# Two mixer layers: a mean in front of half a modulation product, rows copied earlier, two sums of squares in front of another half

## The reference

```python
mod_x = (silu_c @ w_mod[l] + b_mod[l])            # six vectors of 1024: sh1 sc1 gt1 sh2 sc2 gt2
hx = modulate(rms_norm(x, g_norm1[l]), sh1, sc1)
out_x = token_mixer(hx, ...)                      # below
x = x + gt1 * out_x
x = x + gt2 * channel_mixer(modulate(rms_norm(x, g_norm2[l]), sh2, sc2))

def token_mixer(h, p, ...):
    a_val, a_gate, s_bg, s_cg, s_x, c_x, c_g = split(h @ p['w_in'])
    u = conv_a(a_val * sigmoid(a_gate), p['conf_w'], ...)       # 31 taps
    ya = silu(layer_norm(u, ...))                               # mean and variance over 256 channels
    yb = s_bg * conv_b(s_cg * s_x, ...)
    hf, hb = rglru_bidir(c_x, ...)                              # gates, two scans
    yc = (hf + hb) * gelu(c_g)
    y = head_rms_norm(concatenate([ya, yb, yc]), p['g_mix'])    # mean square over heads of 64
    return y @ p['w_out'], ...
```

## Time and profile before

| | before |
|---|---|
| device time, median of 3 runs | 1575.61 us (1571.6 to 1576.92) |
| the profiled execution, device time | 1575.62 us |
| its span in the trace | 1573.5 us |
| TensorE busy | 1485.1 us (94%) |
| VectorE busy | 838.6 us (53%) |
| ScalarE busy | 617.6 us (39%) |
| mean granted TensorE clock | 0.972 |

### The profile page before, as it was taken

The page is one execution under the profiler, slowest core; times in us unless marked ns, Lnnn a source line. Parts: engine busy times, 40 slices in busy tenths (PEclk is TensorE's granted clock), DMA queues, the critical chain, the costliest instruction groups (busy, mean ns, idle before and its releaser), DMA issues.

```text
span 1573.5 us, 21947 instructions
## 1 busy us (share of the span) xinstructions
PE 1485.1 (94%) x8714; PEld 1046.4 (67%) x8715; DVE 838.6 (53%) x1135; ACT 617.6 (39%) x698; POOL 17.4 (1%) x56
## 2 busy tenths in 40 slices
PE   5999798999999999897869999999999999999997
PEld 3886487788888887783745566565666557555764
DVE  2899945333333323798553554445554555545553
ACT  3426723322122222549243333334444444434442
POOL 2000000000000000100010000000000000000000
PEclk8999999999999999899989999999999999999998
DMA  9633933922533133347259999989999999999992
GB/s 359 194 107 111 329 124 135 226 74 57 151 107 91 55 109 124 107 135 275 84 216 346 329 337 328 339 322 407 380 408 407 400 389 398 409 376 406 382 409 110
DMA packets 208007, 395.44 MB, mean 251 GB/s; under 512 B 12045, under 2 KB 123041, under 8 KB 207905
## 3 DMA queue, kind: packets, MB, share of 16 engines
q1 hardware_dynamic: 207312, 393.80, 69.8%
q10 hardware_dynamic: 592, 0.21, 0.1%
HBM read 392.93 MB, written 1.05 MB: 250 GB/s over the span
## 4 chain that ended last, share of the span: by engine, by line
PE 87%; ACT 4%; DMA 4%; DVE 3%; issue 2%; DVEq 0%; ACTq 0%; SPq 0%
PE bank L754 86%; DMA raw<-in_w_mod 2%; PE bank L1244 1%; DMA raw<-in_moe_w 1%; DVE tb L1824 1%; ACT la L1528 1%; DVE h_lo L1832 0%; ACT lr L1522 0%; PE bank L1189 0%; DMA rows_sb<-in_b_mod 0%; PE bank L779 0%; ACT li L1524 0%; ACT lm L1535 0%; ACT w_hi L1407 0%; ACT lr L1530 0%
## 5 line engine op out<-in xcount | busy, mean ns | idle before, releaser
L2261 DVE TENSOR_TENSOR w_lo<-raw,w_hi 128x2048 fp32r<-128x2048 f32 x132 | 302.4, 2291 | 265.8 <-ACT w_hi L1649 263.0
L1649 ACT ACTIVATE w_hi<-raw 128x2048 fp32r<-128x2048 f32 x132 | 252.4, 1912 | 409.6 <-PE bank L754 282.4
L754 PE MATMUL bank<-h_hi,w_hi 128*128 128x512 f32 (+1 forms) x768 | 285.7, 372 | 13.8 <-DVE h_lo L1832 11.8
L754 PE MATMUL bank<-h_lo,w_hi 128*128 128x512 f32 (+1 forms) x768 | 283.6, 369 | 0.0
L754 PE MATMUL bank<-h_hi,w_lo 128*128 128x512 f32 (+1 forms) x768 | 283.6, 369 | 0.0
L1407 ACT ACTIVATE w_hi<-raw 128x2048 fp32r<-128x2048 f32 (+1 forms) x64 | 113.7, 1776 | 211.1 <-PE bank L754 197.7
L754 PEld LDWEIGHTS bank<-h_hi,w_hi 128*128 128x128 f32 x768 | 147.2, 192 | 39.6 <-DVE h_lo L1832 13.4
L754 PEld LDWEIGHTS bank<-h_lo,w_hi 128*128 128x128 f32 x768 | 147.5, 192 | 23.6
L754 PEld LDWEIGHTS bank<-h_hi,w_lo 128*128 128x128 f32 x768 | 147.4, 192 | 23.7
L754 PE MATMUL bank<-w_hi,hc_hi 128*128 128x512 f32 (+1 forms) x384 | 153.8, 401 | 2.5 <-ACT warm L1704 2.5
L1807 DVE TENSOR_TENSOR w_lo<-raw,w_hi 128x2048 fp32r<-128x2048 f32 (+1 forms) x64 | 135.9, 2123 | 36.5 <-ACT w_hi L1407 36.3
(11 more groups left out here) (307 smaller groups left out, 1803.3 us busy)
## 6 DMA issues: line engine op xcount, KB each, us to landing
raw<-in_moe_w SPq DMA_DIRECT2D x220, 1024.0 KB, 8.7
raw<-in_w_mod SPq DMA_DIRECT2D x48, 1024.0 KB, 8.3
raw_x<-in_moe_w SPq DMA_DIRECT2D x44, 1024.0 KB, 8.7
raw<-in_ffn_w SPq DMA_DIRECT2D x44, 512.0 KB, 5.3
raw<-in_w_in SPq DMA_DIRECT2D x18, 1024.0 KB, 5.4
raw<-in_ffn_w SPq DMA_DIRECT2D x16, 704.0 KB, 4.5
raw<-in_w_out SPq DMA_DIRECT2D x8, 1024.0 KB, 5.7
x_in<-in_ctx SPq DMA_DIRECT2D x1, 1024.0 KB, 5.0
```

Source lines behind the costliest of these rows:

```text
L754: return nc.tensor.matmul(dst, lhsT, rhs, start=first, stop=last)
L1649: nc.scalar.activation(w_hi[:, j % SPL, :], raw[:, E_SLOT[j], :], ACT.Copy)\
L2261: V.tensor_tensor(w_lo[:, j % SPL, :], raw[:, E_SLOT[j], :], w_hi[:, j % SPL, :].bitcast(F32), ALU.subtract).then_inc(dve_done, dve_n(name ...
```

## The change

Four edits in the two mixers. No instruction is added or taken away.

1. In layer 1, at gate 4, the mean of the convolution's output comes ahead of the first half of vector 3 on TensorE, not behind it.
2. In layer 0 VectorE copies the rows of vectors 2 and 3 one tile earlier, in tile (1, 1), ahead of the LayerNorm's product (L2096).
3. In layer 1 VectorE copies them two tiles earlier, in tile (1, 0).
4. In both layers TensorE sums the squares of tiles 4 and 5 ahead of the second half of vector 5; tiles 6 and 7 stay behind it.

```diff
                     if q == CONF_AT[l]:
                         head_sums(l, ts, HEAD_SUM[0], (2, 3))
-                    if (l, q) == (1, 4):
-                        modulation(*MIX_MODS[l][0][1], range(2))
                     if q == MEAN_AT[l]:
                         pe.wait_ge(*evacuated(("w_in", l, WIN_ORDER[-1])))
                         pe.wait_ge(dve_done, at("conf_u", l))
                         for v in range(2):
                             i = mm(STAT[:, ts], ones_d[:, :].to_broadcast([P, P]), y[:, v, ts], v == 0, v == 1)
                         i.then_inc(pe_done, pe_n("conf_mean", l))
+                    if (l, q) == (1, 4):
+                        modulation(*MIX_MODS[l][0][1], range(2))
...
                 for i8 in range(4):
                     head_factor(l, ts, i8)
+                head_sums(l, ts, HEAD_SUM[1], (4, 5))
                 modulation(*MIX_MODS[l][1][1], range(2, MOD_K))
-                head_sums(l, ts, HEAD_SUM[1], (4, 5, 6, 7))
+                head_sums(l, ts, HEAD_SUM[1], (6, 7))
...
-                        if (d, t) == (1, 2):
+                        if (d, t) == (1, 1 - l):
                             dve.wait_ge(pe_done, at("used", "mod", *MIX_MODS[l][0][1], MOD_K - 1))
                             for m in MIX_MODS[l][0]:
                                 mod_row(*m)
```

## The result

The changed kernel took 1567.9 us (median of 9 runs, 1566.3 to 1569.72) against 1574.03 us before (9 runs, 1571.17 to 1576.92): a ratio of 0.9958, 95% interval 0.9946 to 0.997, or 6.1 us by the medians and 6.6 us by the ratio (4.7 to 8.5 us by its interval). The forecast was 1571.8 us, 4.0 us less, with 1569.0 as the lower end of its range. The direction was right; the size was too small by about 2 us, and the time fell out of the range.

What follows compares the result with a forecast made beforehand. TensorE, busy 1485.1 of 1573.5 us, was taken as the bound, so only idle or low-clock time could be won. Gains of 2.8 + 1.2 = 4.0 us gave 1571.6, stated as 1571.8 us, range 1569 to 1576.

Steps and rivals of the forecast that it cites:

- The chain: Both mixers: late rows delay vector 4, that delays vector 5's last load, and that the sums and ScalarE's squares (8.27 us idle).
- Layer 1, 2.8 us (2.4 to 3.0): Layer 1's mixer: the first w_out product starts at about 757.3 instead of 760.13, 2.8 us gained.
- the slow sums of tiles 0 and 1: Layer 1, behind the pause: these sums (0.60 us) take up to 0.3 us more at low clock.
- Layer 0, 1.2 us: Layer 0's mixer: first product 0.4 us later, a low-clock stretch worth 1.7 us goes; net 1.2 us gained.
- 0.92 us more at half clock: Layer 0: sums of tiles 0 and 1 take 0.92 us longer, moving tile 7 from 192.60 to 193.5.
- The low-clock stretch: Layer 0, 196.2 to 199.6 at clock 0.50: expected to go because TensorE works without a gap; costs 1.7 us.
- The sum: Whole kernel: 2.8 us from layer 1 plus 1.2 us from layer 0, 4.0 us gained.
- Whatever these two starts gain is kept: After 760.13 (layer 1) and 195.32 (layer 0) TensorE has long product stretches ahead, so gains there stay.
- the clock moves elsewhere in the layers between: Between the mixers: listed as one sign that the prediction is wrong, with no size given.
- The slower one: After the longer pauses TensorE stays at 1.2 GHz through both stretches: 9 us lost, 1584.8 us; chance 0.04.
- More than forecast: Both mixers: new bursts start at full clock and later drops go too, over 4.7 us gained, 1570.5 us; chance 0.1.

Runs made afterwards that it cites:

- the rows alone: Kernel before with only the row copies moved, one tile sooner in layer 0 and two in layer 1: 1572.17 us, ratio 0.9991 to before.
- The delays: Changed kernel plus unread matmuls of 512, 512 + 256 or 3 x 512 columns in layer 0's w_out product: 1568.7, 1570.13 and 1571.36 us.
- the warm pause: Changed kernel plus unread matmuls (6 in layer 0, 8 in layer 1) before the sums of tiles 0 and 1: 1570.18 us, ratio 0.998 to before.

## Why the prediction was right and wrong

**The chain was read rightly.** Late rows, late vector 4, late load, late squares: all four links moved as described. The columns of layer 1 follow the last gate at once, the last chunk of vector 5 is there in time, ScalarE's 8.27 us wait is gone, and the product waits for tile 7.

**Edit 1** gave ScalarE its 0.80 us; the mean waited 0.67 us for the convolution's last tap, as the estimate had it. What the forecast did not see is that this is worth little without edit 4 (50.70 against 50.89 us).

**Layer 1, 2.8 us (2.4 to 3.0).** Against the profile that the forecast was made from it was 52.90 - 49.52 = 3.38 us, against the two later profiles of before 2.0 to 2.2 us. The mechanism was right, and the 2.8 us lie between the two. Part of the base was particular to the profile read: the low-clock stretch from 756.0, which the two later profiles of before do not have. Two details were off: the first product was set by tile 7 alone, not by TensorE's burst, and the slow sums of tiles 0 and 1 cost 0.1 us (0.70 against 0.60), not the 0.3 I allowed.

**Layer 0, 1.2 us.** The first product was to come 0.4 us later. In the profile it came 0.13 us sooner after the first square; beside the two later profiles of before it came 0.2 us later. The step at fault is "0.92 us more at half clock": the sums took 1.13 us instead of 0.92, because those 0.92 us were mostly the wait for the second square, not work. The low-clock stretch went as forecast, worth 1.56 us. The reason given, TensorE at work without a gap, is not shown: with the rows alone this stretch ran at full clock too, though TensorE had waits of 0.59 and 1.08 us right ahead of the first product, as before.

**The sum.** In the profiles the two mixers gave 3.38 + 1.56 + 0.13 = 5.1 us, or, from the later profiles of before, 2.1 + 1.55 - 0.2 = 3.4 us; the forecast of 4.0 lies between. This is the part that the sum had terms for.

**What failed is that the sum ended there.** "Whatever these two starts gain is kept" was true, but not all. The stretches between the mixers were put at nothing, without a reason: the text named "the clock moves elsewhere in the layers between" only as a way to be wrong and gave it no term and no side. The profiles have there 1.6 + 0.9 us less, with 0.6 us more just ahead, 1.9 us in all. Timeline of TensorE at the norm's broadcast, first before, then after:

```profile
633.31 2.08 PE L754 MATMUL bank<-rs,ident 128*128 128x128 f32 x8 [1.54 <-DVE modT L1864]
```

```profile
630.42 1.16 PE L754 MATMUL bank<-rs,ident 128*128 128x128 f32 x8 [1.54 <-DVE modT L1865]
```

The same eight records, behind the same wait, took 2.08 us at half clock and 1.16 at full clock. Stretches of TensorE in both places, of before, and then at the norm, of after:

```profile
288.40:291.80 3.40, 3.40 (x9) 0.50 0.62 160
633.10:643.30 10.20, 7.00 (x31) 0.50 0.01 2
```

```profile
632.40:639.10 6.70, 4.53 (x21) 0.50 0.01 2
```

A stretch of 3.4 us at 0.50 with TensorE busy throughout costs 1.7 us, which is the difference of the first half (114.1 against 112.5). Adding these to the terms: 3.4 to 5.1 us in the mixers and 1.9 us between give 5.3 to 7.0 us, around the measured 5.5 to 6.6. The whole way from the first square to layer 1's first low part took 577.4, 575.8 and 575.4 us in the profiles of before and 570.2 to 570.5 us in the four of after. The delays show that in the profiles a shift in time is enough to bring the 1.9 us back; how much of it is in the median of timed runs stays open.

**The rivals.** The slower one needed a clock that stays low for more than 8.1 us after work resumes. It was 0.50 to about 748.4, 4.7 us after 743.73, within the 3.3 to 6.2 that the old rows gave. (In its strongest form this rival doubles the work: 2 x 6.9 = 13.8 us in layer 1, not the 14.6 it was given, so its loss would be about 8.4 us and not 9.) The price of the slow burst was 0.1 us in layer 1, measured by the warm pause, since the burst had cover. The Trainium skill (TensorE: Matmul & The Clock Gate, "HAM oscillation — how this bites in real kernels") warns of bursts that start slow behind a wait. The trace agrees: behind both longer pauses, of 8.52 and 6.10 us, TensorE worked at 0.50. "More than forecast" had a chance of 0.1, and half of its mechanism ("later drops go too") came about, though without the full clock behind the pauses. It should have had more: the three drops in the earlier trace rows already showed how often they stand in the way.

## What to carry to other kernels

When a wait starts a chain (here rows, then a vector, then a load, then a sum), follow the chain to its end before you price it: it is worth what its last link frees, and no more than the next engine in line lets through. A slow burst behind a pause costs next to nothing while another engine's work covers it (0.1 us in layer 1 here), and a kernel with that pause padded ran slower. Without the cover it costs: with the rows alone, layer 0 took 14.30 us to its first low part, where before took 12.24 to 12.59. When a kernel has low-clock stretches on its path, a shift of a microsecond ahead of them can add or remove one: give them a term and a range on both sides. And profile the kernel before more than once, since a forecast takes its base from one profile: one of the three here had layer 1 longer by 1.2 us than the next.

## What the runs showed of the hardware

In two stretches without a changed instruction the granted clock fell at the same places in every profile of one kernel: 114.07 to 114.14 and 5.05 us in three profiles, 112.48 to 112.51 and 4.13 us in four. That is not so everywhere: of the three profiles of before one alone has the low clock from 756.0 to 759.4, and layer 0 with one and the same program took 12.80 + 23.06 us in one profile and 14.30 + 21.42 us in another. Added matmuls of 0.9 and 1.3 us brought 2.5 us of slower work back in stretches that begin some 60 and 410 us behind them (and took 0.6 us off in front), and 2.6 us of them took it away again. I had taken the places of these stretches for chance.
